# Layer 1's per-head sums in a two-layer mixer trunk: head pattern standing and 512 tokens moving, norms on eight rows

## What is computed

```
kk = kh * rw_k_k.astype(F32).reshape(RW_HEADS, RW_HEAD_DIM)
kk = kk / jnp.maximum(jnp.sqrt(jnp.sum(kk * kk, axis=-1, keepdims=True)), 1e-12)
...
bonus = (jnp.sum(rh * kh * rw_r_k.astype(F32), axis=-1, keepdims=True) * vh).reshape(bsz, T, RW_W)
y_rw = ((yr + bonus) * g).astype(h.dtype)
```

## Time and profile before

| | before |
|---|---|
| median of three runs | 1268.0 us |
| the profiled execution | 1268.96 us, of which its span 1266.9 us |
| PE busy | 1239.4 us, 98% of the span |
| DVE, ACT, POOL busy | 58%, 49%, 46% |
| mean granted TensorE clock | 0.994 |
| PE's share of the chain that ended last | 90% |

### The profile page before, as it was taken

The page is one execution under the profiler, slowest core; times in us unless marked ns, Lnnn a source line. Parts: engine busy times, 40 slices in busy tenths (PEclk is TensorE's granted clock), DMA queues, the critical chain, the costliest instruction groups (busy, mean ns, idle before and its releaser), DMA issues.

```text
span 1266.9 us, 19290 instructions
## 1 busy us (share of the span) xinstructions
PE 1239.4 (98%) x7550; PEld 1052.9 (83%) x7550; DVE 735.4 (58%) x1102; ACT 615.5 (49%) x991; POOL 586.8 (46%) x685
## 2 busy tenths in 40 slices
PE   7999989999999999999999999999999999999997
PEld 5877757888998989987788888888888898998986
DVE  4528676562653725644788887576563472652743
ACT  5345675462452633644583536743554272461641
POOL 5653214766174173563455543331656336165080
PEclk9999999999999999999998999999999999999999
DMA  9332101435252451432213321000335254242311
GB/s 279 93 84 67 51 17 53 114 100 166 67 144 57 114 136 29 122 83 62 72 51 83 84 68 51 2 2 18 107 93 149 67 147 121 65 135 67 100 35 67
DMA packets 173258, 108.40 MB, mean 86 GB/s; under 512 B 4590, under 2 KB 170736, under 8 KB 173168
## 3 DMA queue, kind: packets, MB, share of 16 engines
q1 hardware_dynamic: 172688, 107.09, 29.8%
q0 software_dynamic: 480, 0.08, 0.0%
HBM read 105.05 MB, written 2.10 MB: 85 GB/s over the span
## 4 chain that ended last, share of the span: by engine, by line
PE 90%; DVE 6%; ACT 2%; issue 1%; DMA 0%; DVEq 0%; SPq 0%; ACTq 0%
PE ps L1257 9%; PE ps L1256 9%; PE ps L1258 9%; PE ps L1125 7%; PE ps L1127 7%; PE ps L1126 7%; PE ps L1222 6%; PE ps L1221 6%; PE ps L1220 6%; PE ps L1112 2%; PE ps L1236 2%; PE ps L1235 2%; PE ps L1234 2%; PE ps L1605 1%; PE ps L1175 1%
## 5 line engine op out<-in xcount | busy, mean ns | idle before, releaser
L1014 POOL TENSOR_TENSOR w_lo<-raw_w,w_hi 128x256 fp32r<-128x256 f32 x248 | 212.2, 886 | 261.3 <-ACT w_hi L1761 261.3
L2486 DVE TENSOR_TENSOR h<-h,ps 128x512 f32<-128x512 f32 x64 | 44.0, 687 | 206.5 <-PE ps L1258 206.5
L1125 PE MATMUL ps<-hn_hi,w_hi 128*128 128x512 f32 x368 | 152.3, 414 | 1.0 <-DVEq L2577 1.0
L1127 PE MATMUL ps<-hn_hi,w_lo 128*128 128x512 f32 x368 | 145.8, 396 | 0.0
L1126 PE MATMUL ps<-hn_lo,w_hi 128*128 128x512 f32 x368 | 145.1, 394 | 0.0
L1071 POOL TENSOR_TENSOR wx_lo<-raw_w,wx_hi 128x256 fp32r<-128x256 f32 x128 | 97.8, 796 | 40.1 <-ACT wx_hi L1828 40.1
L1828 ACT ACTIVATE wx_hi<-raw_w 128x1024 fp32r<-128x1024 f32 x62 | 65.4, 1054 | 104.0 <-PE ps L1258 91.4
L1071 POOL TENSOR_TENSOR wx_lo<-y_mix,wx_hi 128x256 fp32r<-128x256 f32 x64 | 51.7, 839 | 135.7 <-ACT wx_hi L1828 135.7
L1828 ACT ACTIVATE w_hi<-raw_w 128x1024 fp32r<-128x1024 f32 x54 | 57.0, 1055 | 110.3 <-PE ps L1258 100.1
L1071 POOL TENSOR_TENSOR w_lo<-raw_w,w_hi 128x256 fp32r<-128x256 f32 x120 | 89.9, 780 | 40.1 <-ACT w_hi L1828 40.1
L1257 PE MATMUL ps<-hid_lo,w_hi 128*128 128x512 f32 x256 | 100.7, 394 | 0.0
(11 more groups left out here) (484 smaller groups left out, 3320.9 us busy)
## 6 DMA issues: line engine op xcount, KB each, us to landing
raw_w<-in_w_up SPq DMA_DIRECT2D x40, 512.0 KB, 4.3
raw_w<-in_w_down SPq DMA_DIRECT2D x40, 512.0 KB, 4.1
raw_w<-in_o_w_in SPq DMA_DIRECT2D x27, 512.0 KB, 3.8
y_mix<-in_w_up SPq DMA_DIRECT2D x24, 512.0 KB, 4.5
y_mix<-in_w_down SPq DMA_DIRECT2D x24, 512.0 KB, 4.6
raw_w<-in_e_w_in SPq DMA_DIRECT2D x19, 512.0 KB, 3.8
raw_w<-in_e_w_out SPq DMA_DIRECT2D x8, 512.0 KB, 3.5
raw_w<-in_o_w_out SPq DMA_DIRECT2D x8, 512.0 KB, 3.5
```

Source lines behind the costliest of these rows:

```text
L1014: nc.gpsimd.tensor_tensor(w_lo[:, n % CUT, ks], raw_w[:, n % RING, ks], w_hi[:, n % CUT, ks].bitcast(F32), ALU.subtract).then_inc(w_cut, 1)
L1125: mm(o, a_hi, b_hi, start=(k == 0), stop=False)
L1127: ins = mm(o, a_lo, b_hi, start=False, stop=(k == KT - 1))
```

## The change

The sums are turned round. Before, 128 tokens of the squares stood in the array (128 by 128) and the heads' pattern of two columns moved, 16 fp32 matmuls for `kk_sum` and 16 for `bonus`; the result had tokens on the partitions, 32 numbers in each. Now the pattern stands, padded to eight columns and shifted by two for each `f`, and 512 tokens move: 4 matmuls, summed in PSUM into rows 0 to 7, one row for each head. The root, the clamp and the reciprocal work on 8 partitions by 512 columns in the first tile of `kk_sq`. Spreading takes 8 matmuls of 512 columns with 8 rows of the array instead of 32 of 128 columns with 128 rows. The bonus gets two steps: `bonus_sum` (the sum, behind slot 13), a copy of the eight rows to SBUF on ACT, and `bonus` (a turn back to tokens on partitions, 4 matmuls with 128 columns standing and 8 moving, behind slot 15). DVE copies the bonus out after `conv_staged(16)` instead of after `conv_staged(13)`. The plan of banks holds one entry more, so later users of the banks move by one.

```diff
-        ("heads", np.stack([_i // 64 == 0, _i // 64 == 1], 1)),
+        ("heads", np.pad(np.stack([_i // 64 == 0, _i // 64 == 1], 1), ((0, 0), (6, 6)))),
...
-              13: [("bonus",)], 14: [("a_turn",)],
+              13: [("bonus_sum",)], 14: [("a_turn",)], 15: [("bonus",)],
...
-        kk_norm = tiny(NT, 8)
+        kk_norm = kk_sq[0:8, 0, :]
+        bonus_rows = mats_rk[0:8, 0, :]
...
-                    elif kind == "kk_sum":
-                        o = free(pe, "kk_sum")
+                    elif kind in ("kk_sum", "bonus_sum"):
+                        o = free(pe, kind)
                         for f in range(4):
-                            pe.wait_ge(S["kk_sq"], f + 1)
-                            for t in range(NT):
-                                c = 8 * t + 2 * f
-                                ins = mm(o[:, c:c + 2], kk_sq[:, f, t * P:(t + 1) * P], const("heads"),
-                                         start=True, stop=True)
-                        close(ins, "kk_sum")
+                            pe.wait_ge(S["kk_sq" if kind == "kk_sum" else "rk_ready"], f + 1)
+                            src = kk_sq if kind == "kk_sum" else mats_rk
+                            ins = mm(o[0:8, :], const("heads")[:, 6 - 2 * f:14 - 2 * f], src[:, f, :],
+                                     start=(f == 0), stop=(f == 3))
+                        close(ins, kind)
...
-                        for t in range(NT):
-                            for par in range(2):
-                                hh = 2 * f + par
-                                ins = mm(o[64 * par:64 * par + 64, t * P:(t + 1) * P],
-                                         kk_norm[:, t, hh:hh + 1].to_broadcast([P, 64]), ident,
-                                         start=True, stop=True, skip_group_check=True)
+                        for par in range(2):
+                            hh = 2 * f + par
+                            ins = mm(o[64 * par:64 * par + 64, :], ident[0:8, hh:hh + 1].to_broadcast([8, 64]), kk_norm,
+                                     start=True, stop=True, skip_group_check=True)
...
                     elif kind == "bonus":
-                        pe.wait_ge(S["rk_ready"], 4)
+                        drained(pe, "bonus_sum")
                         o = free(pe, "bonus")
-                        heads = const("heads")
                         for t in range(NT):
-                            for f in range(4):
-                                ins = mm(o[:, t * 8 + 2 * f:t * 8 + 2 * f + 2], mats_rk[:, f, t * P:(t + 1) * P], heads,
-                                         start=True, stop=True)
+                            ins = mm(o[:, t * 8:t * 8 + 8], bonus_rows[:, t * P:(t + 1) * P], ident[0:8, 0:8],
+                                     start=True, stop=True)
...
-                    A(kk_norm.rearrange("p n c -> p (n c)"), o[:, 0:32], ACT.Sqrt).then_inc(free_sem("kk_sum"), 1)
+                    A(kk_norm, o[0:8, :], ACT.Sqrt).then_inc(free_sem("kk_sum"), 1)
...
+                if j == 13:
+                    drain(bonus_rows, "bonus_sum", src=bank(("bonus_sum",))[0:8, :])
                 if j == 14:
-                    full(act, "bonus")
...
-                if i == 13:
+                if i == 16:
                     o = full(dve, "bonus")
```

## The result

The changed kernel takes 1290.95 us (median; runs of 1284.76, 1285.59, 1296.31 and 1298.3) against 1267.77 of before, run beside it: ratio 1.0184, 95% interval 1.0158 to 1.0210. The forecast was 1270.9 with a range up to 1274.4. The sign was right and the size far off. Even the spread is new: the kernel of before stays within 1265 to 1271 in every set of runs here. The changed kernel's runs lie in two groups, near 1285 and near 1297, and its median lies between them, where no run does.

A forecast was written before the change was run, and what follows sets the result against it. PE was taken as the bound, busy for 98% of the span, except between slots 7 and 8. Terms 3.8 - 0.15 + 1.7 - 2.4 = +2.9 on the median 1268.0 gave 1270.9 us, range 1268.8 to 1274.4.

The forecast's parts named there:

- What else hangs on it: Later DVE work behind the reciprocal, the moved bonus copy and the shifted banks: all priced at 0.
- `kk_sum`: 0: The sum of the squares: 3.5 us against 3.57, and a clock staying high behind it gains nothing.
- R3: Rival: `bonus_sum` still lowers the clock, so its gains in slot 14 and the sum vanish; 1274.1 us, chance 0.12.
- The chain, +3.8: Root, clamp and reciprocal ahead of `kk_inv` grow from 32 to 512 columns: +0.49, +0.30 and +3.00 us.
- R4: Rival: root, clamp and reciprocal on eight rows are priced by their elements, so faster; 1265.4 us, chance 0.05.
- `kk_inv`, -0.15: Spreading the norms: two halves of the array run side by side, 3.5 us against 3.65 before.
- R5: Rival: the two halves of `kk_inv` don't run side by side, +3.4; 1274.3 us, chance 0.06.
- The clock behind the wait, +1.7: After PE idles 6.8 us ahead of `kk_inv`, 3.4 us of dense work run at half clock; bounds 0 and 3.3.
- R2: Rival: eight rows don't wake the clock, so `kk_inv` runs at half clock throughout; 1274.4 us, chance 0.12.
- `bonus`, -2.4: Bonus sum and slots 14 to 15: sum -1.2, slot 14 at normal clock -2.0, the turn behind slot 15 +0.9.

The follow-up runs named there:

- all tiles moved: The kernel of before with an unused tile of 12 columns in front of all other tiles: 1268.27 us, ratio 1.0000.
- 448 bytes: The kernel of before with an unused tile of 112 columns ahead of `hn`: 1267.85 us.
- placed by the table: The kernel of before with unused tiles of 48 columns ahead of `d_hi`, 128 ahead of `hn`, 112 ahead of `hid`: 1265.62 us; with the changed bonus too, 1265.97.

## Why the prediction was wrong, step by step

The 23.2 us over before, part by part, each by the difference of two medians:

| part | forecast | measured | from |
|---|---|---|---|
| bonus | -2.4 | -0.8 | bonus alone, placed as before, against before |
| `kk_sum` to slot 8 | +5.35 | +8.5 | change placed as before, against bonus alone |
| distance of matmuls | none | +9.0 | change with gaps in POOL's train, against change placed as before |
| long DVE operations | none | +5.9 | change, against the same with gaps |

The parts sum to 22.6; another 0.5 is the difference between the medians of before in the two sets of runs (1268.24 and 1267.77). The last part is the median of four runs in two groups: an execution pays nothing or about 12.

- **"What else hangs on it", 0: this is the step that failed**, by 14.9 us. I went through queues and banks and left out memory. The wider table was in the diff, and the trace of before couldn't price it, but that every later tile moves against `w_hi` could be seen. None of the rivals held it, so the range had no place for it. What the runs showed in its place: a slower stream of matmuls, 9.0 us, and long DVE operations, 5.9. The clock term failed beside it, and alone it would have been enough for a miss: in place, the kernel still took 1275.98, 7.7 over before, where 2.9 was forecast.
- *`kk_sum`: 0* held. The sum took 3.53, and no low clock followed. R3 is out for both sums.
- *The chain, +3.8*: right. Root 0.59 (0.69 forecast), clamp 0.41 (0.48), reciprocal 3.34 (3.35). The way from the start of `kk_sum` to that of `kk_inv` grew by 3.33 (15.43 against 12.10 in the earlier trace rows), 3.56 in the kernel placed as before. The 4.3 that I had estimated from the Trainium skill (VectorE: DVE Perf Modes, "First, the fixed hardware budget") for the reciprocal is out: 3.34 on 8 partitions, 3.35 on 128. So is R4.
- *`kk_inv`, -0.15*: the halves do run side by side: eight pairs in 7.02 at half clock are 0.88 each, which would be 0.44 at full clock. R5 is out. But all of it ran at 1.2 GHz, so the term was +3.37.
- *The clock behind the wait, +1.7*: mis-sized. R2 was the true case, with a chance of 0.12: low in all of `kk_inv` and for nine or ten matmuls of slot 8, 0.43 in place of 0.23 each. With +3.37 and about +1.8 that is 5.2 where R2 had 5.15 and the forecast 1.55; with the chain's 3.56 it makes 8.7, near the 8.5 measured. R2's 1274.4 lies 1.6 below the 1275.98 of the placed kernel, which is what the bonus didn't bring. I had priced the low clock from one execution, and it is no fixed thing: over the 20 profiles the 2.96 us stretch of layer 0 was followed by it in 16, and the 2.26 us stretch, which I took for safe, in 11.
- *`bonus`, -2.4*: too much. The stretch had 1.9 less against the profile of before, but that gain isn't there in every execution. From the start of `bonus` to the start of the transposes behind it (703.81 before) it took 28.9 us there, with the clock low for 6.8 us behind `bonus`. Eight profiles have this order of work: the clock was low for 6.8 us in four of them and for 3.4 in the other four, and three of the latter (all tiles moved, 448 bytes, placed by the table) took 27.3 to 27.4. The kernels with the changed bonus take 26.9 (placed as before) and 27.3 (placed by the table). So the gain is 2.0 or 0.4, or nothing, by the state of the clock; the measured -0.8 and, placed by the table, +0.35 can't be told from zero.

What is not settled: why the distance of two tiles sets the pace; why the clock fell or not behind the same idle stretch from one execution to the next; and what sets off a long DVE operation. Without the gaps in POOL's train they stand in five of the eleven profiles with a slower matmul stream and in none of the eight at 0.2289 and less. A shifted phase between POOL and DVE is my guess; no run shows it.

## What to carry to other kernels

A change that widens one table moves every tile behind it. List the addresses of standing and moving tiles before and after, and if they moved against each other, hold them in place with padding before judging the change itself; here the artefact was twice the size of the effect. Count what an idle stretch costs in clock together with the work that follows it: thin matmuls right behind the wait let the low clock run on for their whole length (back after 8.6 to 13.0 us with eight rows, after 3.8 and 6.0 with 128). And take a gain that rests on the end of a low-clock stretch from several profiles, not one.

## What the hardware showed that I had not expected

- Matmuls of 512 columns in the same program start 0.2269 to 0.2343 us apart, by the distance of the standing from the moving tile: 3%. With 256 columns it is 5.7% (0.1135 to 0.1200), and there the distance isn't all.
- A DVE operation of 0.69 us stood for 8.14 beside a seamless train of POOL operations; a wait between these, which made POOL no bottleneck, took 5.9 us off the median.
- The clock stayed at 1.2 GHz for 11.0 us after PE had begun again with eight-row matmuls, and 12 profiles with the new sums (128 rows and eight columns standing, 512 columns moving) have no low clock behind `bonus_sum`, where two moving columns brought it every time.
- The same idle stretch of 2.3 us in layer 0 was followed by the low clock in 11 of 20 profiles and not in the other 9.
